# Rotary embedding of an encoder layer: halves swapped by transfers inside SBUF in place of products with a permutation

## What is computed

```python
def partial_rope(x, pos):
    half = ROPE_DIM // 2                      # 8
    ...
    xr = x[..., :ROPE_DIM].astype(F32)
    x1, x2 = xr[..., :half], xr[..., half:]
    rot = jnp.concatenate([x1 * cos - x2 * sin, x2 * cos + x1 * sin], axis=-1).astype(x.dtype)
    return jnp.concatenate([rot, x[..., ROPE_DIM:]], axis=-1)

q = partial_rope(proj[..., OFF_AQ:OFF_AK].reshape(B, S, A_HEADS, A_HEAD_DIM), pos)
k = partial_rope(proj[..., OFF_AK:OFF_AV].reshape(B, S, A_KV_HEADS, A_HEAD_DIM), pos)
...
attn = windowed_gqa(q, k, v, attn_sink)
```

## Time and profile before

| | us |
|---|---|
| median of three runs | 790.04 |
| lowest, highest | 788.25, 791.03 |
| the profiled execution | 790.24 |
| its span, first to last instruction | 788.4 |
| PE busy (share of the span) | 705.0 (89%) |
| DVE busy | 516.1 (65%) |
| ACT busy | 396.9 (50%) |
| POOL busy | 200.2 (25%) |

### The profile page before, as it was taken

One profiled execution on the slowest core, in us unless ns is written; L12 is line 12 of the kernel. 1 busy time (PEld: TensorE's weight loads), 2 busy tenths in 40 slices (PEclk: granted clock), 3 DMA queues, 4 the chain that ended last, 5 costly groups with the idle time before them and its releaser, 6 DMA issues.

```text
span 788.4 us, 9856 instructions
## 1 busy us (share of the span) xinstructions
PE 705.0 (89%) x3662; PEld 563.1 (71%) x3662; DVE 516.1 (65%) x655; ACT 396.9 (50%) x488; POOL 200.2 (25%) x107
## 2 busy tenths in 40 slices
PE   3699999999999999999996789999999999999810
PEld 2376777777878888888886668877787777778600
DVE  2545734703544645968058888888888888888636
ACT  4341225133553637233143477777767666777423
POOL 0002433332313323469430111321112121200040
PEclk9999999999999999999996699999999999999965
DMA  9993677659208421786505699999999999994162
GB/s 314 300 267 88 205 234 238 225 165 255 66 25 281 100 74 54 240 263 221 199 28 213 251 368 366 383 391 384 375 373 368 378 370 381 378 361 165 60 231 116
DMA packets 79615, 192.22 MB, mean 244 GB/s; under 512 B 14350, under 2 KB 55574, under 8 KB 73436
## 3 DMA queue, kind: packets, MB, share of 16 engines
q1 hardware_dynamic: 72196, 169.86, 61.9%
q0 software_dynamic: 4272, 11.31, 4.1%
q10 hardware_dynamic: 3112, 10.59, 3.3%
HBM read 179.10 MB, written 16.83 MB: 249 GB/s over the span
## 4 chain that ended last, share of the span: by engine, by line
PE 43%; DVE 26%; issue 15%; ACT 8%; SPq 3%; DMA 2%; ACTq 1%; POOLq 0%; POOL 0%; DVEq 0%
PE psum L819 33%; DVE moe_low L2226 14%; ACT half_high L1524 3%; PE psum L903 2%; ACT xbuf L1435 2%; DVE xsT_low L2236 2%; ACT xbuf L1443 2%; PE psum L1070 1%; PE psum L889 1%; SPq L671 1%; DMA rot_pT<-ada_w 1%; DVE xbuf L1859 1%; DVE stat L1864 1%; DVE oT L2245 1%; PE psum L1093 1%
## 5 line engine op out<-in xcount | busy, mean ns | idle before, releaser
L2339 POOL TENSOR_TENSOR low_ring<-front_ring,high_ring 128x1024 fp32r<-128x1024 f32 x49 | 120.4, 2462 | 260.0 <-ACT high_ring L1340 260.0
L1340 ACT ACTIVATE high_ring<-front_ring 128x1024 fp32r<-128x1024 f32 x51 | 53.9, 1056 | 172.6 <-PE psum L819 123.4
L2226 DVE TENSOR_TENSOR moe_low<-front_ring,half_high 128x2048 fp32r<-128x2048 f32 x48 | 107.9, 2286 | 10.2 <-ACT half_high L1524 10.2
L819 PE MATMUL psum<-half_high,xsT_low 128*128 128x512 f32 x256 | 103.8, 405 | 9.4 <-DVE xsT_low L2236 9.4
L819 PE MATMUL psum<-h_low,high_ring 128*128 128x512 f32 x288 | 107.2, 390 | 0.0
L819 PE MATMUL psum<-moe_low,xsT_high 128*128 128x512 f32 x256 | 101.8, 398 | 0.0
L819 PE MATMUL psum<-half_high,xsT_high 128*128 128x512 f32 x256 | 101.5, 397 | 0.0
L1524 ACT ACTIVATE half_high<-front_ring 128x2048 fp32r<-128x2048 f32 x48 | 91.0, 1917 | 6.4 <-PE psum L819 6.0
L819 PE MATMUL psum<-h_high,low_ring 128*128 128x512 f32 x224 | 91.3, 407 | 1.2 <-DVE low_ring L1727 1.2
L819 PE MATMUL psum<-h_high,high_ring 128*128 128x512 f32 x224 | 87.4, 390 | 0.0
L2226 DVE TENSOR_TENSOR moe_low<-slots,half_high 128x2048 fp32r<-128x2048 f32 x32 | 73.1, 2287 | 8.2 <-ACT half_high L1524 8.2
(11 more groups left out here) (310 smaller groups left out, 1275.6 us busy)
## 6 DMA issues: line engine op xcount, KB each, us to landing
front_ring<-w_down SPq DMA_DIRECT2D x16, 2048.0 KB, 10.8
front_ring<-w_in SPq DMA_DIRECT2D x34, 512.0 KB, 6.1
xbuf<-ada_w SPq DMA_DIRECT2D x32, 512.0 KB, 4.3
slot<-w_gate SPq DMA_DIRECT2D x8, 2048.0 KB, 9.8
front_ring<-w_up SPq DMA_DIRECT2D x8, 2048.0 KB, 9.8
slots<-w_up SPq DMA_DIRECT2D x8, 2048.0 KB, 9.8
slots<-w_gate SPq DMA_DIRECT2D x8, 2048.0 KB, 9.6
y_rows<-inout ACTq DMA_DIRECT2D x16, 512.0 KB, 9.6
```

The source lines that it names most:

```text
L819: mm = pe.matmul(out, lhs(a, k), rhs(b, k), start=(start and k == 0 and a == 1), stop=(stop and k == count - 1 and (a, b) == (0, 0)))
L1340: act.activation(dst, src.rearrange("p (k n) -> p k n", k=KD), ACT.Copy).then_inc(high_ready, 1)
L2226: dve.tensor_tensor(low_of(slot, h), half_of(slot, h), half_high[place].bitcast(F32), ALU.subtract).then_inc(low_dve, 1)
L2339: pool.tensor_tensor(low, src, high.bitcast(F32), ALU.subtract).then_inc(low_ready, 1)
```

## The change

The five products with the permutation go, with their PSUM groups. Behind each copy of raw n, ACT issues four transfers inside SBUF: for each of the two heads, partitions 0 to 7 to partitions 8 to 15 of another tile, and 8 to 15 to 0 to 7, each eight partitions by 2 KB. The tile (`swapped`, two of them, in a region that is used later) is cleared once by POOL at the start. DVE waits for the four transfers of its n in place of the product, and counts finished rotations with a semaphore of their own; ACT's copies from n = 2 on and PE's first scores wait for that count.

```diff
-    steps, turn = [("swap", 0), ("values", None), ("swap", 1)], None
+    steps, turn = [("rope", 0), ("values", None), ("rope", 1)], None
...
-        g += {"piece": lambda: finished_by(*what), "swap": lambda: [(f"swap{what}", "v")],
+        g += {"piece": lambda: finished_by(*what), "rope": lambda: [],
...
+        swapped = [hm[:, 2 + n, :] for n in range(2)]
...
-            def swap(n):
-
-                wait_bank(pe, f"swap{n}")
-                wait_emptied(pe, f"raw{n}")
-                pe.matmul(bank(f"swap{n}"), perm, raw[n % 2], start=True, stop=True).then_inc(psum_full, 1)
-
...
-                if kind == "swap":
-                    swap(what)
+                if kind == "rope":
+                    continue
...
                 if b == 0:
-                    wait_emptied(pe, "swap4")
+                    pe.wait_ge(rope_done, 5)
...
             def copy_raw(n):
                 wait_full(act, f"raw{n}")
                 if n >= 2:
-                    wait_emptied(act, f"swap{n - 2}")
+                    act.wait_ge(rope_done, n - 1)
                 act.activation(raw[n % 2], bank(f"raw{n}"), ACT.Copy).then_inc(act_emptied, 1)
+                if n == 0:
+                    act.wait_ge(swap_cleared, 1)
+                wait_emptied(act, f"raw{n}")
+                for base in (0, A_HD):
+                    for to, at in ((base, base + HALF), (base + HALF, base)):
+                        act.dma_start(swapped[n % 2][to:to + HALF, :], raw[n % 2][at:at + HALF, :]
+                                      ).then_inc(swap_landed[n], 16)
...
                 link(dve.tensor_tensor(two(rot[:, n, :]), two(raw[n % 2]), table("cos"), ALU.mult))
-                wait_full(dve, f"swap{n}")
-                link(dve.tensor_tensor(two(tmp[:, :]), two(bank(f"swap{n}")), table("sin"), ALU.mult))
-                emptied(dve.tensor_tensor(rot[:, n, :], rot[:, n, :], tmp[:, :], ALU.add))
-                wait_emptied(dve, f"swap{n}")
+                dve.wait_ge(swap_landed[n], 16 * 4)
+                link(dve.tensor_tensor(two(tmp[:, :]), two(swapped[n % 2]), table("sin"), ALU.mult))
+                dve.tensor_tensor(rot[:, n, :], rot[:, n, :], tmp[:, :], ALU.add).then_inc(rope_done, 1)
+                dve.wait_ge(rope_done, n + 1)
...
             pool.memset(row_terms, 0.0).then_inc(terms_cleared, 1)
+            pool.memset(hm[:, 2:4, :], 0.0).then_inc(swap_cleared, 1)
```

More of the change, by code:

```diff
@@ L45 @@
 A_HEADS, A_KV, A_HD = 8, 2, 64
+HALF = 8
 PAIRS = A_HEADS // A_KV
@@ L139, in projection_steps @@
         if name == "aq":
-            steps.append(("swap", j))
+            steps.append(("rope", j))
         elif (name, j) == ("mq", 0):
-            steps.append(("swap", 4))
+            steps.append(("rope", 4))
             steps.append(("gates", None))
@@ L470, in hybrid_layer @@
         conv_done = sem("conv_done")
+        swap_cleared = sem("swap_cleared")
+        swap_landed = [sem(f"swap_landed{n}") for n in range(5)]
+        rope_done = sem("rope_done")
         forget_abs = sem("forget_abs")
```

## The result

Of 20 runs each the changed kernel took 791.57 us at the median (789.88 to 795.35) and the kernel before 789.88 us (788.25 to 791.24). The ratio is 1.0028, with a 95% interval of 1.0017 to 1.0038: slower by 0.28%, or 1.7 us, which is clear of the noise and within the 0.3% that the prediction called no change. One run of a later experiment, e3_both, was in a slow state, at 1437.41 us, and is left out of its numbers. The profiled execution took 793.18 us with a span of 791.3 us. The lines of its trace that answer to those of before follow; code lines of the changed kernel are its own (L824 the split matmuls, L1382 the issues of the transfers, L894 the transposes).

What follows compares the result with a forecast made beforehand. PE's order was taken to bound the projections, with the chain going through DVE and ACT from the scores on. -4.30 + 0.85 + 1.86 + 1.57 = -0.02 us on 790.24 gave 790.2 us, range 787.8 to 793.5.

Steps and rivals of the forecast that it cites:

- The products, -4.30: In PE's projections: removing five permutation products of 0.86 us each takes 4.30 us off PE's chain.
- The issues on ACT's queue, +0.85: Behind raw 0's copy: four issues of 0.35 us delay vT, returning 0.85 us; at 0.78 us an issue, 2.57 us.
- ACT is held longer: Rival at the values: issues of 0.78 us give 791.9 us, of 1.73 us 795.6; chance 0.12, half beyond 792.6.
- 0.26 us for issues of 0.227 us: Lower case at the values: with 0.227 us an issue, 0.26 us of the products' saving is given back.
- 795.6 for 1.73 us: Upper case of the longer ACT hold at the values: 1.73 us an issue would give 795.6 us in all.
- The clock: Rival: half clock behind the pauses at mv0 and scores, 1.6 us each; 793.4 us for both (chance 0.08), 791.8 one (0.10).
- The banks, +1.86 and +1.57: Moved PSUM banks make PE wait 1.86 us at mv0 for DVE's conv7, 1.57 us at the first scores for ACT's mo1.
- a shift at 200 us should stand in the end: Stages behind the scores, routing then experts, start from earlier results, so a shift there carries through to the total time.
- The landings, 0: Arrival of raw 0's transfers, between nothing and 6.2 us after issue, is covered at the first rotation and costs nothing.
- DVE, 0: Sine product reading SBUF twice may take 1.77 us more in each of five rotations, but DVE's slack makes it free.
- if the clock is at 0.50 behind one, or if vT ends after 62 us: Signs of being wrong: half clock behind the pause at mv0 or the scores, or vT, expected near 60.8 us, ending after 62.
- within 0.3 us of where they stood: Sign at the first attention scores: they start within 0.3 us of their time in the kernel before.

Runs made afterwards that it cites:

- e3_both: Changed kernel with the earlier kernel's PSUM banks and raw 0's transfers issued behind the copy vT: 785.81 us in five runs, ratio 0.9946 to the kernel before.
- e5_no_swap: Changed kernel without transfers or products, sine product reading raw itself, banks of the kernel before: 785.63 us, ratio 0.9951 to the kernel before.
- e2_order: Changed kernel with raw 0's four transfers issued behind the copy vT, not ahead of the split before it: 788.06 us, ratio 0.999 to the kernel before.
- e7_fill: Changed kernel with eight more PE matmuls ahead of the transposes of vT, in the pause for the values: 790.66 us, ratio 1.002 to the kernel before.
- e1_banks: Changed kernel with the PSUM banks of the kernel before, the five products' groups still counted: 788.65 us, ratio 0.9982 to the kernel before.
- e4_banks_alone: Kernel before, products kept in banks 6 and 7, all other groups in the changed kernel's banks: 793.22 us, ratio 1.0037 to the kernel before.

## Why the prediction was right, and where it wasn't

The time was right: 790.2 forecast, 791.57 measured, inside the range and within 0.3% of before. Its sum wasn't: it had -0.02 us at the first scores, and the traces have +3.3. Carried to the end, the terms as measured give 790.24 + 3.35 = 793.6 us, just outside the range of 787.8 to 793.5; the time lies in it by luck, because about half of the loss came back behind the scores.

- *The products, -4.30:* right (4.26 in e5_no_swap).
- *The issues on ACT's queue, +0.85: this is the step that failed.* The term was mis-sized. I took 0.35 us an issue from the ACT transfer with as many rows; measured are 0.63 to 0.80 us, so that ACT is held for 3.20 us and PE for 2.46 us, near the 2.57 us that the text gave for 0.78 us. The upper of the two ACT rows was the better one, and the rival that came was "ACT is held longer". (By the text's own terms its 0.26 us for issues of 0.227 us should be 0.36, and its 795.6 for 1.73 us should be 795.7; the sum uses neither.) The order that makes it (split 5, then vT, behind the issues) was right, as e2_order shows.
- *The clock:* it fell, as in the rival, but not where the rival had it. I had put it to the pauses at mv0 and at the scores, and not asked what a longer pause at the values would do to it. The failed term thus cost twice: 1.61 us of pause and 1.62 us behind it, of which e7_fill puts 1.41 to the half clock. Behind the two pauses that the text did name the clock held in all four traces of the changed kernel. The Trainium skill ("TensorE: Matmul & The Clock Gate", section "HAM oscillation — how this bites in real kernels") has pauses between matmul groups put the next group at the half clock; here that held behind each pause of 2.4 to 2.6 us at the values, and behind only two of eight of 1.93 us at mv0.
- *The banks, +1.86 and +1.57:* right, 1.93 and 1.64 us, at the places and by the releasers named; e1_banks and e4_banks_alone show each half by itself. They were to be had from the code alone, though the diff doesn't show them; without them the sum would have been 786.8 us.
- *The stages behind the scores, "a shift at 200 us should stand in the end":* it didn't. Of the 3.3 us at the first scores 1.7 stand in the medians, and in e4_banks_alone 3.5 of 5.3. I had taken the stages behind the scores to last as long from a later start; with the clock at the places in the table above they differ by up to 3.6 us between traces.
- *The landings, 0:* right. The last issue of raw 0 ended at 60.82, and DVE's sine product began at 62.26, at most 1.44 us later, far from the 6.2 us of the upper end.
- *DVE, 0:* right. The first sine product took 2.71 us with POOL at a low part from 62.06 to 64.42 us, the second 0.69 us. ACT's copy of raw 2 waited for the end of the first rotation (2.83 us, before the change 3.49), but PE had no pause from either.
- *What I said would show me wrong:* "if the clock is at 0.50 behind one, or if vT ends after 62 us". vT ended at 62.47. The first scores, which were to be within 0.3 us of where they stood, came 3.3 us later.

## What to carry to other kernels

When a product becomes a transfer, the transfer's own time may be hidden, but its issue stands in some engine's order: put it behind the work that the bottleneck is waiting for. And when results leave PSUM, count anew which bank each later one gets; here two waits of 1.93 and 1.64 us came from that, and giving the banks back took 3.35 us off the stretch ahead of the scores. A pause on TensorE that grows past the ones seen to be harmless should be priced with the clock behind it.

## What the runs showed of the hardware

- An issue by ACT of a transfer of eight rows inside SBUF takes 0.63 us at the median and up to 0.80 us, with rows of 2 KB or of 1 KB alike (3.20 and 3.13 us for four).
- It doesn't stop activations that ACT has already been given: a split of 1.05 us and a copy of 0.59 us ran beside the issues in e2_order.
- The clock by the length of the pause ahead, in the traces of these kernels: it fell behind all six of 2.4 to 2.6 us at the values and behind every one of 2.65 us in the first expert; behind 2.83 to 2.88 us in the last expert it fell in ten traces of fourteen; behind 1.93 us at mv0 in two of eight, and behind 1.64 us at the scores in none of eight. So a pause's length alone doesn't tell it.
